# Norm's factor multiplied in after the product, weight halves renumbered, two steps of the scan moved: a hybrid decoder step on one core

## The reference, cut to what matters

```python
def rmsnorm(x, g):
    return x * rsqrt(mean(x * x, axis=-1) + 1e-5) * g
a = rmsnorm(h, norm_mix[0]);  h += ssd_mixer(a)                 # norm 0, scan, gating, ssd_w_out
a = rmsnorm(h, norm_ffn[0])                                     # norm 1
gu = a @ ffn_w_gu;            h += (silu(gu[:2816]) * gu[2816:]) @ ffn_w_down
a = rmsnorm(h, norm_mix[1])                                     # norm 2
u, v = split(gelu(a @ sgu_w_in + b_in));  v = layernorm(v)
h += (u * (tril(w_s) @ v + b_s)) @ sgu_w_out
a = rmsnorm(h, norm_ffn[1]);  h += moe_top2_of_8(a)             # norm 3
y = rmsnorm(h, norm_final)
```

## Time and profile before

| | |
|---|---|
| median of three runs | 1757.13 us |
| profiled execution, its own time | 1755.17 us |
| its span | 1753.4 us |
| PE busy | 1642.4 us (94%) |
| DVE busy | 1355.4 us (77%) |
| ACT busy | 1089.4 us (62%) |
| DMA | 494.98 MB, 282 GB/s over the span |

### The profile page before, as it was taken

One profiled execution on the slowest core, in us unless ns is written; L12 is line 12 of the kernel. 1 busy time (PEld: TensorE's weight loads), 2 busy tenths in 40 slices (PEclk: granted clock), 3 DMA queues, 4 the chain that ended last, 5 costly groups with the idle time before them and its releaser, 6 DMA issues.

```text
span 1753.4 us, 25753 instructions
## 1 busy us (share of the span) xinstructions
PE 1642.4 (94%) x9328; PEld 1409.4 (80%) x9328; DVE 1355.4 (77%) x1716; ACT 1089.4 (62%) x1121; POOL 95.3 (5%) x89
## 2 busy tenths in 40 slices
PE   5899779699998999799999999999999999999994
PEld 4888668599998999678888888888888888888883
DVE  5787776467766665588798798899888887988895
ACT  5554443356664444377677777777777776776774
POOL 0012100111210000000000000000000000000000
PEclk9999889799999999899999999999999999999997
DMA  5476538299997553389999999999999999999995
GB/s 162 137 189 154 146 98 227 48 276 266 257 298 238 164 149 115 133 317 375 355 387 361 348 396 356 364 384 351 379 378 352 377 374 356 386 359 351 393 356 179
DMA packets 264105, 494.98 MB, mean 282 GB/s; under 512 B 11126, under 2 KB 168054, under 8 KB 263729
## 3 DMA queue, kind: packets, MB, share of 16 engines
q1 hardware_dynamic: 249792, 456.39, 74.3%
q0 software_dynamic: 8400, 30.25, 7.5%
q10 hardware_dynamic: 5844, 7.41, 1.3%
HBM read 476.38 MB, written 17.83 MB: 282 GB/s over the span
## 4 chain that ended last, share of the span: by engine, by line
PE 76%; DVE 2%; ACT 1%; DMA 1%; issue 0%; DVEq 0%; ACTq 0%; SPq 0%; POOLq 0%
PE bank L1375 12%; PE bank L1377 12%; PE bank L1376 12%; PE bank L986 6%; PE bank L987 6%; PE bank L1397 6%; PE bank L1396 6%; PE bank L1398 6%; PE bank L988 6%; PE bank L1349 1%; PE bank L1243 1%; PE bank L1320 0%; ACT part L395 0%; DVE raw_r L402 0%; PE bank L976 0%
## 5 line engine op out<-in xcount | busy, mean ns | idle before, releaser
L2052 DVE TENSOR_TENSOR raw_r<-raw_w,part 128x2048 fp32r<-128x2048 f32 x336 | 759.4, 2289 | 128.3 <-ACT part L899 118.6
L899 ACT ACTIVATE part<-raw_w 128x2048 fp32r<-128x2048 f32 x336 | 636.4, 1917 | 156.0 <-DMA raw_w<-in_moe_w_gu_dram 114.9
L1375 PE MATMUL bank<-part,xh 128*128 128x512 f32 x896 | 357.5, 399 | 1.7 <-DVE xl L2007 1.7
L1377 PE MATMUL bank<-part,xl 128*128 128x512 f32 x896 | 353.9, 395 | 0.0
L1376 PE MATMUL bank<-raw_r,xh 128*128 128x512 f32 x896 | 353.8, 395 | 0.0
L986 PE MATMUL bank<-ah,part 128*128 128x264 f32 x928 | 276.5, 298 | 10.7 <-DVE al L1435 8.5
L988 PE MATMUL bank<-al,part 128*128 128x264 f32 x928 | 267.2, 288 | 0.0
L402 DVE TENSOR_TENSOR raw_r<-raw_w,part 128x2048 fp32r<-128x2048 f32 (+1 forms) x65 | 137.5, 2127 | 95.5 <-ACT part L395 94.8
L1375 PEld LDWEIGHTS bank<-part,xh 128*128 128x128 f32 x896 | 168.0, 187 | 41.2 <-issue 1.9
L1377 PEld LDWEIGHTS bank<-part,xl 128*128 128x128 f32 x896 | 167.9, 187 | 41.0
L1376 PEld LDWEIGHTS bank<-raw_r,xh 128*128 128x128 f32 x896 | 168.1, 188 | 39.1
(11 more groups left out here) (392 smaller groups left out, 2129.5 us busy)
## 6 DMA issues: line engine op xcount, KB each, us to landing
raw_w<-in_moe_w_gu_dram SPq DMA_DIRECT2D x227, 1024.0 KB, 5.6
raw_w<-in_moe_w_down_dram SPq DMA_DIRECT2D x112, 1024.0 KB, 5.0
raw_w<-in_ffn_w_gu_dram SPq DMA_DIRECT2D x44, 512.0 KB, 8.2
raw_w<-in_ssd_w_in_dram SPq DMA_DIRECT2D x20, 1024.0 KB, 5.4
raw_w<-in_sgu_w_in_dram SPq DMA_DIRECT2D x16, 1024.0 KB, 5.7
raw_w<-in_ffn_w_down_dram SPq DMA_DIRECT2D x16, 704.0 KB, 7.8
raw_w<-in_state_ssm_dram SPq DMA_DIRECT2D x16, 512.0 KB, 6.6
raw_w<-in_ssd_w_out_dram SPq DMA_DIRECT2D x8, 1024.0 KB, 5.7
```

The source lines that it names most:

```text
L899: act.activation(first_half(ND + n, 0, SLOT), raw_w[:, q, :], ACT.Copy).then_inc(S("part1"), 1)
L1375: mm(out, xh[:, k, :], w[0][:, kk, c], start=(k == 0), stop=False)
L1377: ins = mm(out, xl[:, k, :], w[0][:, kk, c], start=False, stop=(k == DT - 1))
L2052: tt(second_half(ND + n, 0, SLOT), raw_w[:, q, :], first_half(ND + n, 0, SLOT).bitcast(F32), ALU.subtract).then_inc(S("part2"), 1)
```

## The change

1. **Norm's factor.** For norms 1 and 2, ACT and DVE make halves of x times g, without the factor, tile by tile while the projection is still running (`squares`, `plain_2`). PE multiplies the first 4 dense tiles with these: two pairs of the dense SwiGLU (`LATE_F = 2`) and four tiles of `sgu_w_in` (`LATE_S = 4`, in banks 0 to 3). DVE multiplies their sums by the factor on the way out of PSUM (semaphore `late`), and Silu and Gelu then work in place. Later tiles use normed halves as before, written over the plain ones as the last plain tile has read them (`plain_used`). The last `sum_square` of the norm stands inside the first dense tile, before its last k.
2. **High buffers.** `hi_slot` is shifted by 2, so that tiles 28 and 29 take the buffers of tile 25, and 30 and 31 those of tile 26. Weight halves are made three tiles ahead in place of two from tile 28 on; the third half ahead of the experts moves into the last projection.
3. **Scan.** Tanh stands before the copy of the state. `mean_square` moves to the end of t = 5, 9, 13; root, reciprocal, scaling, first halves and rests move one iteration earlier.
4. **Around them.** The conv rows go out two at a time after m = 2, 3, 4. The state update runs from the sixth pair on, 20 halves in 17 pairs. Turning and masking of the spatial weights moves behind the fifth gating tile, and v tiles 0 to 7 are turned two at a time after tiles 5 to 8. Two semaphores are merged.

In the diff `pe`, `act` and `dve` name the engine; `mixing` masks the spatial weights, which stood ahead of the gating loop before.

```diff
+LATE_F = 2
+LATE_S = 4
         def hi_slot(n):
-            return (n - SSD_TILES) % HI
+            return (n - SSD_TILES + 2) % HI
+        def plain_at(n, k):
+            return DT + 2 * DT * (n - 1) + k + 1
+        def normed_at(n, k):
+            return 2 * DT + 2 * DT * (n - 1) + k + 1
+        def turned_v(n):
+            if LATE_S < n < LATE_S + 5:
+                return [2 * (n - LATE_S) - 2, 2 * (n - LATE_S) - 1]
+            return [n - 1] if LATE_S + 5 <= n <= IT else []
+        def halves_done(n):
+            return max(n - 5, 0) * 20 // 17
...
 +            def squares(n, before_, ahead):
                 for m in range(DT):
                     ahead(m)
                     act.wait_ge(S("x_ready"), DT * n + m + 1)
                     act.wait_ge(S("sq_used"), DT * (n - 1) + before_ + m - 1)
                     act.activation(sq[:, m % 2, :], xT[:, m, :], ACT.Square).then_inc(S("sq_ready"), 1)
+                    if n < 3:
+                        c = NORM[n] + m
+                        act.activation(ah[:, m, :], xT[:, m, :], ACT.Copy, scale=V[:, c:c + 1]).then_inc(S("a1"), 1)
                 act.wait_ge(S("ms_ready"), n + 1)
                 act.activation(rs[:, 1, :], rs[:, 0, :], ACT.Sqrt).then_inc(S("root_ready"), 1)
+            def normed_1(n):
+                for m in nk:
+                    act.wait_ge(S("a_ready"), DT * (n - 1) + m + 1)
+                    if m < DT - 1:
+                        act.wait_ge(S("plain_used"), (DT - 1) * (n - 1) + m + 1)
+                    elif n == 1:
+                        act.wait_ge(S("ffn"), LATE_F)
+                    else:
+                        act.wait_ge(S("sgu"), LATE_S)
+                    act.activation(ah[:, m, :], aT[:, m, :], ACT.Copy).then_inc(S("a1"), 1)
...
-                if t % 4 == 0 and t < IT:
-                    act.wait_ge(S("misc"), 4 + 2 * g + 1)
-                    act.activation(hp, psum[5][:, :], ACT.Copy).then_inc(S("misc_free"), 1)
                 if t < IT:
                     (tanh of t)
+                if t % 4 == 0 and t < IT:
+                    act.wait_ge(S("misc"), 4 + 2 * g + 1)
+                    act.activation(hp, psum[5][:, :], ACT.Copy).then_inc(S("misc_free"), 1)
-                if t == 11:
+                if t == 10:
                     (root of groups 0 and 1)
-                if 13 <= t:
-                    first_parts(2 * t - 26, 2 * t - 24)
+                if 12 <= t < IT:
+                    first_parts(2 * t - 24, 2 * t - 22)
...
+            def ahead_out(m):
+                if m:
+                    split_1(act, 22 + m)
+                if m == DT - 1:
+                    split_1(act, 23 + m)
+            squares(1, IT, ahead_out)
...
 -                    split_1(act, SSD_TILES + n + 2)
-                    act.wait_ge(S("ffn"), n + 1)
+                    split_1(act, SSD_TILES + n + 3)
+                    if n >= LATE_F:
+                        act.wait_ge(S("ffn"), n + 1)
+                    if n == LATE_F - 1:
+                        normed_1(1)
+                    if n < LATE_F:
+                        act.wait_ge(S("late"), n + 1)
...
 +            def tile_of(bank, w, c, n, u, late):
+                kt = w[0].shape[1]
+                for k in range(kt):
+                    if u == 0:
+                        pe.wait_ge(S("a2"), plain_at(n, k))
+                        if k == kt - 1:
+                            sum_square(n, IT, DT - 1)
+                    if u == late:
+                        pe.wait_ge(S("a2"), normed_at(n, k))
+                    ins = product(psum[bank][:, 0:T], [u_[:, k, c:c + P] for u_ in w], [u_[:, k, :] for u_ in a12],
+                                  k == 0, k == kt - 1)
+                    if u == late - 1 and k < kt - 1:
+                        ins.then_inc(S("plain_used"), 1)
+                return ins
             n0 = SSD_TILES
+            pe.wait_ge(S("x_ready"), 2 * DT)
             for p in range(FT):
...
 # VectorE
-                if t == 6:
-                    mean_square(0)
-                if t == 10:
-                    mean_square(1)
-                if t == 14:
-                    mean_square(2)
-                if t == 12:
+                if t in (5, 9, 13):
+                    mean_square(t // 4 - 1)
+                if t == 11:
                     dve.wait_ge(S("groot_ready"), 1)
                     own.did(dve.reciprocal(rs[:, :, :], rs[:, :, :]))
-                if 12 <= t < 16:
-                    scaled(2 * t - 24)
-                    scaled(2 * t - 23)
-                if 13 <= t:
-                    second_part_z(2 * t - 26)
-                    second_part_z(2 * t - 25)
+                if 11 <= t < 15:
+                    scaled(2 * t - 22)
+                    scaled(2 * t - 21)
+                if 12 <= t < IT:
+                    second_part_z(2 * t - 24)
+                    second_part_z(2 * t - 23)
...
 +                    if n == LATE_F - 1:
+                        normed_2(1)
+                    if n < LATE_F:
+                        dve.wait_ge(S("ffn"), n + 1)
+                        tt(fs[:, n % 2, :], psum[2 * (n % 2)][:, 0:T], rsq, ALU.mult).then_inc(S("late"), 1)
+                        step(tt(hf[:, n % 2, :], up, rsq, ALU.mult))
                     tt(hf[:, n % 2, :], fs[:, n % 2, :], up, ALU.mult).then_inc(S("ffn_h"), 1)
+                    split_2(dve, SSD_TILES + n + 3)
...
 -                if n % 2 == 0 and n < 2 * IT:
-                    split_2(dve, U0 + n // 2 + 2)
+                if n % 2 == 0 and LATE_S <= n < 2 * IT:
+                    split_2(dve, U0 + n // 2 + 3)
+                if n == LATE_S - 1:
+                    normed_2(2)
+                if n < LATE_S:
+                    dve.wait_ge(S("sgu"), n + 1)
+                    tt(vT[:, n, :], psum[n][:, 0:T], rsq, ALU.mult).then_inc(S("late"), 1)
+                if n == LATE_S - 1:
+                    for k in range(LATE_S // 2):
+                        split_2(dve, U0 + k + 3)
+                if n == LATE_S:
+                    mixing()
+                    small_rows()
```

More of the change, by code:

```diff
@@ L657, in _, with squares @@
             split_1(act, 1)
-            def norm(n, before_, ahead=lambda m: None):
+            def squares(n, before_, ahead):
                 for m in range(DT):
@@ L815, in ahead_down @@
                         act.dma_start(bsr[8 * k:8 * k + 8, :], i["sgu_b_s"][0]).then_inc(S("late_in"), 16)
-            norm(2, IT, ahead_down)
+            squares(2, IT, ahead_down)
             U0 = D0 + 16
@@ L853, in _ @@
             act.dma_start(wr, i["moe_w_router"][0].rearrange("(k p) e -> p k e", p=P)).then_inc(S("late_in"), 16)
-            norm(3, IT, lambda m: split_1(act, U0 + 16 + m + 2))
-            for k in range(2, AHEAD):
-                split_1(act, ND + k)
+            squares(3, IT, lambda m: split_1(act, U0 + 16 + m + 3))
             act.dma_start(grow, i["norm_final"].unsqueeze(0).to_broadcast((P, D))).then_inc(S("grow_in"), 16)
@@ L999, in _, with tile_of @@
             a12 = (ah, al)
-            def normed(n, first):
-                return lambda k: pe.wait_ge(S("a2"), DT * n + k + 1) if first else None
+            def tile_of(bank, w, c, n, u, late):
+                kt = w[0].shape[1]
[11 more added lines that the diff above has]
+                return ins
             pe.wait_ge(S("wdt2"), 1)
@@ L1212, in _ @@
                 for u in range(2):
-                    ins = dense_tile(2 * (p % 2) + u, w, P * u, a12, ready=normed(1, p == 0 and u == 0))
+                    ins = tile_of(2 * (p % 2) + u, w, P * u, 1, 2 * p + u, 2 * LATE_F)
                 ins.then_inc(S("ffn"), 1)
@@ L1218, in _, with mixing @@
             n0 += FT + 16
[L1220 to L1224, removed]
+            pe.wait_ge(S("x_ready"), 3 * DT)
+            def mixing():
+                pe.wait_ge(S("late_in"), 48)
+                for half in range(2):
+                    for g in range(4):
+                        ins = tr(psum[4 + half][:, P * g:P * g + P], wsr[:, 4 * half + g, :], ident[:, :])
+                    ins.then_inc(S("ws_tr"), 1)
             def vtr(t):
@@ L1249, in _ @@
                     w = weight(n0 + n // 2)
[L1250 to L1255, removed]
+                if n >= LATE_S:
+                    pe.wait_ge(S("gelu"), n - 1 if n >= LATE_S + 2 else n - LATE_S + 1)
+                tile_of(n if n < LATE_S else n % 2, w, P * (n % 2), 2, n, LATE_S).then_inc(S("sgu"), 1)
+                if n == LATE_S:
+                    mixing()
+                for t in turned_v(n):
+                    vtr(t)
+                if n == LATE_S + 2:
                     pe.wait_ge(S("bs_ready"), 1)
@@ L1714, in residual @@
                     tt(xT[:, m, :], xT[:, m, :], psum[m % 2][:, 0:T], ALU.add).then_inc(S("x_ready"), 1)
+                    if m and n < 3:
+                        plain_2(n, m - 1)
                 dve.wait_ge(S("x_ready"), DT * (n + 1))
```

(4 more changed lines are left out.)

136 lines of the change are left out of this document (77 added, 59 removed).

## The result

The changed kernel took 1728.62 us (median of 4 runs, 1727.4 to 1733.58) against 1756.39 (1755.42 to 1757.6, 4 runs) for the kernel before: a ratio of 0.985, 95% interval 0.983 to 0.987, 27.8 us less. The forecast was 1722 in a range of 1710 to 1736. The profiled execution took 1728.97 with a span of 1727.2, 26.2 less than the span before.

A forecast was written before the change was run, and what follows sets the result against it. PE was taken as the bound, with losses to win where it stands: scan 16.5, norm 1 18.5, norm 2 0, together 35 us. 1757.13 - 35 = 1722 us, range 1710 to 1736.

The forecast's parts named there:

- Scan: Scan loop: waits removed less added work, 6.9 + 11.0 - 1.6 = 16.3, taken as a gain of 16.5 us.
- DVE as the one bound: Scan, 160.29 to 190.75: freed of waits, DVE's own length of 25.3 us bounds; what PE saves beyond is idle.
- the three waits of z_out go: 11.0: Scan: with tanh ahead of the state copy, DVE's three waits for the tanh vanish, 11.0 us.
- ACT's place at t = 10: Scan: despite root and two table loads, ACT has the exponentials of t = 11 about 0.8 us before DVE asks.
- Norm 1: After norm 1: PE restarts at E + 1.3, third pair ends at about E + 20.5; gain 18.5 us.
- Dense stage: Dense SwiGLU: PE stays without a gap, so its length doesn't change and earlier shifts count in full.
- C: Dense SwiGLU: loads hold it, so norm 1's 18.5 us is given back, 1740 us; chance 0.05.
- D: Dense SwiGLU, pairs 5 to 21: DVE becomes the bound, 3 us more a pair, 1773 us; chance 0.05.
- PE starts at E2 + 0.5: After norm 2: PE starts 0.5 us after E2, the end of its last dense SwiGLU product.
- The gain of 0: After norm 2: tile 9 starts at E2 + 39.5 to 40 against 39.75 before, so no gain (ends -3 and 9).
- strict order on DVE eats the gain: After norm 2: DVE's rests, masking and copies in order make PE wait, taking the 9 us of PE's own count.
- rival A: After norm 2: start of gating is hidden after all, 9 us more gain, 1713 us; chance 0.13.

The follow-up runs named there:

- e9: The changed kernel with the samples' sums of the scan taken over 64 of 128 elements, the other half left out; 1723.69 us.
- e6: The changed kernel with the last of two weight rests ahead of the last add of norms 1 and 2 moved behind it; 1725.24 us.
- e7: The changed kernel with both edits, DVE's order after norm 2 changed and the last add ahead of the last rest; 1717.30 us.
- the second profile: The changed kernel measured once more with nothing edited; 1730.51 us.
- e4: The changed kernel with DVE's masking of the spatial weights behind the first of three weight rests in place of the third; 1733.48 us.
- e5: The changed kernel with masking behind the first weight rest after norm 2 and the next rests one by one behind v tile copies; 1720.45 us.
- e1: The changed kernel with the copy of the state ahead of the tanh again; 1729.23 us.
- e10: The changed kernel with both scan moves undone: tanh behind the state copy, means and their chain one iteration later; 1745.85 us.

## Why the prediction was right, and where its steps were not

- **Scan: right sum, wrong terms.** 17.5 against 16.5. Counted from the first log_decay, z_out(8) comes at 55.2 and z_out(12) at 84.7; the four iterations between z_out(4) and z_out(8) take 25.1 us where I had counted 25.3. DVE as the one bound is half right: PE, of which the prediction said that what it saves is idle again, is busy for all of these 25.1, and DVE's length alone counts only behind z_out(12) (e9). And the step "the three waits of z_out go: 11.0" gave the tanh what the means had earned. Measured, the tanh is worth 2.95 once the means have moved, the means 9.5 to 14.4 in place of 5.3. Two lines of a wait list added up, though the second was the echo of the first two iterations later. The sum came out because both were removed, so that it didn't matter which of them got what, and because it was checked against DVE's length and not only against the waits.
- **ACT's place at t = 10: right.** The timeline of ACT in the changed kernel:

```profile
202.54 1.28 ACT L798 ACT_TABLE_LOAD   x1
203.84 0.65 ACT L798 ACTIVATE rs<-rs 128x528 f32<-128x528 f32 x1
204.50 1.28 ACT L767 ACT_TABLE_LOAD   x1
205.79 0.38 ACT L767 ACTIVATE arena<-bank 128x256 f32<-128x256 f32 x1
```

  Each activation starts 0.01 to 0.02 after its load ends, and the second load 0.01 after the root ends. DVE asks for the exponentials at 208.07, after they are done (207.21). The drain that the Trainium skill ("ScalarE: Activation LUTs", What ACT_TABLE_LOAD costs) adds to a load, which by the prediction's estimate would have cost 2, isn't in the trace; the measurement decides.
- **From the scan to E: costed at nothing, cost 1.3.** All 24 transposes of the conv rows now lie inside the projection; before, the last four stood behind E. Eight take 0.87 us (272.08 to 272.95), so four more are 0.4, and the second eight take 0.9 more than that, with a wait of 0.59 for DVE's copy.
- **Norm 1: right**, 17.8 against 18.5. PE restarts at E + 2.0, not E + 1.3: the prediction counts the two rests ahead of the last add, but lets the second start with its half done, where it waits for the first rest, and the halves start 1.3 after tile 6's end, not 0.85. With one rest behind the add (e6) it is E + 0.7.
- **Dense stage: right**, 177.05 and 177.06 us; rivals C and D are out.
- **Norm 2: the step that failed is "PE starts at E2 + 0.5".** It took the last add to wait for PE alone, as it did before. But the adds of the dense SwiGLU run 2.7 to 5.5 us behind PE in the changed kernel, and the last two weight halves start only when the late add of tile 6 is done, so that their rests end 2.7 after E2. The traces show ACT waiting for the states' loads ahead of these adds, which it didn't before; the update now starts at the sixth pair, in place of the third, but no run undoes that alone, so how much of the delay is due to it isn't shown. That one rest less ahead of the add helps is shown (e6, e7). PE started at E2 + 3.1, tile 4 is 2.6 and the first v turn 1.8 later than forecast, and after that PE ran at the lower level (0.42 us a row in place of 0.28 from 534.4 to 537.1). The gain of 0 became -3.9, and -6.8 in the second profile (46.8 against 39.9), below the lower end of -3. The reason given for the rest, that strict order on DVE eats the gain, held (e4, e5). That PE alone would have reached tile 9 at E2 + 31 is nearly what e7 shows, E2 + 34.1: with another order on DVE rival A comes true.
- **Ahead of the scan and in the experts: not of the change.** 2.5 and 1.7 us in this one execution. Both are the clock; the first is shown below. The experts have the same 4368 matmuls, and in e1 to e10 the stretch takes 1001.5 to 1001.8. In this execution seven rows of 0.63, where the others have 0.40, come 1.6 us behind a stop of 1.85 (the others' stops there are of 1.65 to 1.80), with a slower row at either end; they make 1.6 of the 1.7:

```profile
723.88 0.49 PE L1443 MATMUL bank<-part,xh 128*128 128x512 f32 x1 [1.85 <-DVE xl L2108]
...
725.44 0.63 PE L1443 MATMUL bank<-part,xh 128*128 128x512 f32 x1
```

In the profiled execution the gain is so 8.8 short of 35: norm 2 3.9, the clock ahead of the scan 2.5 and in the experts 1.7, the conv rows 1.3, norm 1 0.7, less the scan's 1.0 and 0.3 behind tile 9. By the medians it is 7.2 short, and as the kernel before came out 0.7 faster than the median that the forecast started from, the time missed by 6.6.

## What to carry to other kernels

Waits of one loop are not independent terms: ask for each wait whether its releaser was late because of another one on the list, and size the sum by the length of the engine that is left as the bound. When work is pulled forward, look at what stands ahead of the last small instruction that another engine waits for, and whether its engine is still on time when it gets there; here a weight rest that PE needed only two weight tiles later stood ahead of an add of 0.42 us and held PE for 1.3 us after norm 1 and some 1.5 to 2 after norm 2. A wait that only moves when its releaser is moved forward (e4) says that more than the one releaser stands in the way; here it helped to push back work that nobody needs yet (e5).

## What the hardware showed that was not expected

The same stop of PE doesn't always cost the same. In the changed kernel a stop of 1.51 us in the first projection was followed by rows of 0.42, the lower level, until 80.2; in the same kernel's second profile the same stop of 1.51 was followed by rows of 0.28. That is 1.2 of the 2.18 us by which the first log_decay started earlier there, at 131.21 in place of 133.39; the other 1.0 lies at the start, where rows of 0.42 last until 32.1 in the first profile and until 29.7 in the second. First profile, then second:

```profile
75.92 0.39 PE L1102 MATMUL bank<-scratch 32*128 32x16 f32 x2 [1.51 <-DVEq L1634]
...
77.16 0.42 PE L1035 MATMUL bank<-ah,part 128*128 128x264 f32 x1
```

```profile
74.94 0.39 PE L1102 MATMUL bank<-scratch 32*128 32x16 f32 x2 [1.51 <-DVEq L1634]
...
76.02 0.28 PE L1035 MATMUL bank<-ah,part 128*128 128x264 f32 x1
```

Of the twelve profiles, that of the kernel before with them, seven have rows of 0.42 behind that stop, and five have at most one. After norm 2 it went the other way: a stop of 2.54 left the four plain tiles at full clock in the first profile (12.3 us), one of 2.94 put them at a granted clock of 0.88 in the second (13.9). These two stops differ in length, but a stop of 2.89 in e1 was followed by full clock and one of 2.78 in e5 by 0.86:

```profile
509.67:521.97 12.30, 12.30 (x98) 12.04 (x98) 7.42 (x15) 8.15 (x9) 0.00 (x0) 1.00 0.68 217
509.19:521.49 12.30, 12.30 (x87) 12.09 (x88) 7.42 (x15) 6.68 (x9) 0.00 (x0) 0.86 0.66 207
```

The Trainium skill ("TensorE: Matmul & The Clock Gate", Part 1: The HAM clock gate) says that the number of slow matmuls differs from run to run of one kernel at its start; the traces here show the like after stops in the middle. A stage that restarts PE after a stop was so worth 1.2 to 1.6 us more or less in one profile than in another, and a variant's stage is better compared with several profiles than with one.
